# Rotated queries and keys of the second attention: transposed on TensorE, or in 32x32 blocks by VectorE with DMAs through device memory

## The chip, the cores and the metric

The kernel runs on one core of one Trainium2 chip. The metric is the device time of one execution, in microseconds (us). The kernel before takes 1788.93 us, the median of three runs (1788.12 to 1791.05).

## The reference

Two transformer blocks, one after the other, over 256 tokens of 2048 columns, all in float32. The change lies in the second block, where one wide product gives queries, keys and values of two attentions ("moba" and "dsa", eight heads of 128 each). Queries and keys are rotated before they are multiplied with each other:

```python
def _rope(x):                       # x: (1, T, heads, 128), T = 256
    half = dh // 2
    ang = arange(T)[:, None] * inv_freq[None, :]
    x1, x2 = x[..., :half], x[..., half:]
    return concatenate([x1 * cos(ang) - x2 * sin(ang), x2 * cos(ang) + x1 * sin(ang)], axis=-1)

proj = h @ w_in                     # 256 x 2048 times 2048 x 11344
ya = _moba_attention(_rope(qa), _rope(ka), va) @ w_moba_out
yb = _dsa_attention(_rope(qb), _rope(kb), vb, q_idx, k_idx, p_wi) @ w_dsa_out
y = (sigmoid(ga) * ya + sigmoid(gb) * yb) @ w_o
```

For each head the attention is softmax(q k^T / sqrt(128) + mask) v. TensorE sums over the partitions of both its operands, so q k^T needs queries and keys with the head's 128 features on the partitions. The projection leaves them with tokens on the partitions. Something has to transpose them, and that is what the change replaces.

## The kernel before

**Products.** Every product of activations with weights is made of three matmuls: each float32 operand is split into a high part, which the matmul takes as it is, and the rest, and high x high, high x low and low x high are summed (`three`, L1539 to L1542). The weights pass in *units* of 512 KB: two blocks of 128 rows by 512 columns. Eight units make a *turn*, in which one block of 512 output columns is made for both tiles of 128 tokens. The program has 76 turns, so 608 units, of 12 matmuls each. A turn's result lies in two PSUM banks, one for each token tile (`PAIR_A` or `PAIR_B`, in alternation).

**The path of a unit.** SyncE (SP) loads it into one of four slots of `raw` (L372), once VectorE is done with the unit four before it (semaphore `lo_ready`). ScalarE (ACT) writes the high part `w_hi` (L562), once TensorE (PE) is done with the unit four before it (`mm_done`). VectorE (DVE) subtracts and writes `w_lo` (L971). Then PE may start. In the programs of ACT and DVE the split of a unit stands three units ahead of PE's (`AHEAD = 3`): in the loop round s of a turn they split unit s + 3, and units 0 to 2 of the next turn are split in rounds 5 to 7.

**The groups.** The heads of both attentions go in four groups g = 0 to 3 of four heads. A group has three turns: queries (part 0, in `PAIR_B`), keys (part 1, `PAIR_A`), values (part 2, `PAIR_B`), that is turns 16 + 3g, 17 + 3g and 18 + 3g. At the end of parts 0 and 1, DVE rotates the result (`rope_chunk`, then `rope`): per token tile two products into `rope_a`, two into `rope_b`, two sums into `rot` (L1271, L1273, L1279). In the next turn, after PE's unit 3, PE turns the 2 x 4 blocks of 128 x 128 of `rot` into two banks (`turn_qk`, through `turn_rows`, L1586), and ACT copies them to `q2_t` or `k2_t` (`keep_qk`, L825). The attention of group g, `attn2(g, k)`, stands between the units 1 to 6 of the following turn, which is part 0 of group g + 1, or the first gate turn. Its first instruction on PE waits for `qk_ready`.

**What sets the order.** Everything is written out by hand: each engine has its own program, in the order in which the functions are called, and semaphores join them. DMAs are issued by SP (weights and all that concerns the kernel's own buffers) and GpSimd (POOL: `ada_raw`, the modulation weights, 512 KB each, which DVE adds up in L978). An engine's waits stand in its program, so all that is behind a wait waits too. That is so on SP as well: a DMA's wait is made before it is issued, and the loads behind it come later.

**The same way elsewhere.** In the feed-forward stage a 256 x 512 result goes this way already: DVE transposes it in 32x32 blocks (L1478), SP writes it to `f_home` in device memory (`write_f`, L436, a row of 4 KB per partition), and reads it back with the blocks in their places (`read_f`, L444, four DMAs of 128 KB in runs of 1 KB). The write is issued after the load of unit 1 of a turn and the read after that of unit 4.

## Time and profile before

| what | value |
| --- | --- |
| median of three runs | 1788.93 us |
| the profiled execution, its own time | 1789.1 us |
| its span in the trace | 1787.4 us |
| TensorE busy | 1772.0 us, 99% |
| VectorE busy | 1255.9 us, 70% |
| ScalarE busy | 898.2 us, 50% |
| GpSimd busy | 124.1 us, 7% |
| granted TensorE clock | 0.999 of full speed (2.4 GHz) |
| share of DMA engines busy in 40 slices | 0.5 to 0.9 |

The span is the time from the program's first instruction to its last. The median was 0.2 us under the profiled execution's time, so differences read from the trace can be set against either. The groups stand in the span from about 421 us (queries of group 0) to about 710 us; their last attention ends in the first gate turn, near 730 us.

### The profile page before, as it was taken

The page shows a single profiled execution, that of the slowest core. Times are in us where ns is not written, and L with a number is a line of the kernel's source. Part 1 is how long each engine was busy: PE and PEld are TensorE (multiplying, and loading weights), DVE is VectorE, ACT ScalarE, POOL GpSimd, SP SyncE. Part 2 cuts the span into 40 slices and gives each one's busy share as a digit, 9 for nine tenths or more (in the row PEclk, how much of TensorE's full clock was granted, in tenths as well). Part 3 has the DMA queues.
Part 4 walks back from the last instruction along what each step waited for, and adds up shares of the span by engine and source line. Part 5 has one row for each costly group of instructions (what it writes and reads, how often), then busy time and mean ns, then how long its engine had stood idle before and what let it go on. Part 6 is the DMA issues. An engine that isn't in the chain of part 4 may idle for free.

```text
span 1787.4 us, 25539 instructions
## 1 busy us (share of the span) xinstructions
PE 1772.0 (99%) x8266; PEld 1456.0 (81%) x8266; DVE 1255.9 (70%) x1685; ACT 898.2 (50%) x1273; POOL 124.1 (7%) x217
## 2 busy tenths in 40 slices
PE   9999999999999999999999999999999999999998
PEld 7777778887888888888888888888888888888886
DVE  5677779778877877777677868777775654545545
ACT  6766675545445454544444545444444444444443
POOL 1011101010000000210001101000000000000000
PEclk9999999999999999999999999999999999999999
DMA  9778778555667768698888966999998865555554
GB/s 354 250 260 282 237 279 314 205 186 172 212 216 243 245 212 293 208 319 284 283 282 289 308 224 211 333 307 319 315 294 241 237 220 191 195 192 193 193 191 139
DMA packets 192894, 443.78 MB, mean 248 GB/s; under 512 B 16849, under 2 KB 25537, under 8 KB 192449
## 3 DMA queue, kind: packets, MB, share of 16 engines
q1 hardware_dynamic: 164384, 339.08, 58.1%
q0 software_dynamic: 28304, 103.89, 17.8%
q8 instruction: 34, 0.56, 0.1%
q14 instruction: 28, 0.22, 0.0%
q10 hardware_dynamic: 144, 0.03, 0.0%
HBM read 432.46 MB, written 10.49 MB: 248 GB/s over the span
## 4 chain that ended last, share of the span: by engine, by line
PE 95%; DMA 2%; DVE 2%; ACT 1%; SPq 0%; issue 0%; DVEq 0%; ACTq 0%
PE bank L1540 30%; PE bank L1542 30%; PE bank L1541 30%; DMA raw<-in_w_in_a 2%; PE bank L1586 1%; PE bank L1710 1%; PE bank L1693 1%; DVE w_lo L971 0%; PE bank L1803 0%; PE bank L1685 0%; PE bank L1809 0%; PE bank L1682 0%; DVE x L998 0%; PE bank L1566 0%; ACT y L566 0%; PE bank L1815 0%
## 5 line engine op out<-in xcount | busy, mean ns | idle before, releaser
L971 DVE TENSOR_TENSOR w_lo<-raw,w_hi 128x1024 fp32r<-128x1024 f32 x605 | 728.9, 1210 | 415.4 <-ACT w_hi L562 413.6
L562 ACT ACTIVATE w_hi<-raw 128x1024 fp32r<-128x1024 f32 x605 | 633.4, 1050 | 709.0 <-PE bank L1542 653.3
L1540 PE MATMUL bank<-w_hi,h_hi 128*128 128x512 f32 x2272 | 895.8, 394 | 3.4 <-DVE w_lo L1081 1.8
L1542 PE MATMUL bank<-w_hi,h_lo 128*128 128x512 f32 x2272 | 885.3, 390 | 0.0
L1541 PE MATMUL bank<-w_lo,h_hi 128*128 128x512 f32 x2272 | 884.5, 389 | 0.0
L1540 PEld LDWEIGHTS bank<-w_hi,h_hi 128*128 128x128 f32 x2272 | 426.7, 188 | 95.5 <-issue 7.2
L1542 PEld LDWEIGHTS bank<-w_hi,h_lo 128*128 128x128 f32 x2272 | 426.5, 188 | 90.2
L1541 PEld LDWEIGHTS bank<-w_lo,h_hi 128*128 128x128 f32 x2272 | 427.0, 188 | 85.1
L978 DVE SCALAR_TENSOR_TENSOR acc_a<-ada_raw,cond,acc_a 128x1024 f32<-128x1024 f32 x112 | 143.3, 1279 | 12.1 <-DMA ada_raw<-in_w_ada 11.9
L487 POOL DMA_DIRECT2D ada_raw<-in_w_ada x160 | 84.7, 529 | 955.7 <-DVE acc_a L978 710.0
L978 DVE SCALAR_TENSOR_TENSOR acc_b<-ada_raw,cond,acc_b 128x1024 f32<-128x1024 f32 x48 | 64.3, 1340 | 1.3 <-DMA ada_raw<-in_w_ada 1.3
L1540 PE MATMUL bank<-w_hi,o_hi 128*128 128x512 f32 x128 | 49.8, 389 | 0.0
L1541 PE MATMUL bank<-w_lo,o_hi 128*128 128x512 f32 x128 | 49.8, 389 | 0.0
L1542 PE MATMUL bank<-w_hi,o_lo 128*128 128x512 f32 x128 | 49.8, 389 | 0.0
L1163 DVE CUSTOM_DVE_ANT_0 s<-bank,bias 128x128 f32<-128x128 f32 x64 | 20.2, 354 | 33.6 <-issue 21.1
L715 ACT ACTIVATE s<-s,neg_cur 128x128 f32<-128x128 f32 x32 | 12.8, 401 | 31.1 <-DVE neg_cur L1168 30.9
L1540 PEld LDWEIGHTS bank<-w_hi,o_hi 128*128 128x128 f32 x128 | 24.0, 188 | 5.0
L1541 PEld LDWEIGHTS bank<-w_lo,o_hi 128*128 128x128 f32 x128 | 24.0, 188 | 5.0
L1542 PEld LDWEIGHTS bank<-w_hi,o_lo 128*128 128x128 f32 x128 | 24.0, 188 | 5.0
L923 ACT ACTIVATE acc_b<-bank 128x512 f32<-128x512 f32 x32 | 19.2, 600 | 17.5 <-PE bank L1542 17.5
L1478 DVE STREAM_TRANSPOSE acc_b<-acc_b 128x512 f32<-128x512 f32 x32 | 22.8, 712 | 1.1
L487 POOL DMA_DIRECT2D ada_more<-in_w_ada x32 | 16.9, 528 | 84.4 <-DVE acc_a L978 44.4
(206 smaller groups left out, 938.1 us busy)
## 6 DMA issues: line engine op xcount, KB each, us to landing
raw<-in_w_ff SPq DMA_DIRECT2D x256, 512.0 KB, 4.5
raw<-in_w_in SPq DMA_DIRECT2D x176, 512.0 KB, 4.5
ada_raw<-in_w_ada POOLq DMA_DIRECT2D x160, 512.0 KB, 5.0
raw<-in_w_in_a SPq DMA_DIRECT2D x69, 512.0 KB, 5.3
ada_more<-in_w_ada POOLq DMA_DIRECT2D x32, 512.0 KB, 6.0
raw<-in_w_out_a SPq DMA_DIRECT2D x32, 512.0 KB, 5.6
raw<-in_w_o SPq DMA_DIRECT2D x32, 512.0 KB, 5.6
raw<-in_w_moba SPq DMA_DIRECT2D x16, 512.0 KB, 4.3
```

The lines of the kernel that those rows point to most:

```text
L487: pool.dma_start(two(ada_slot(slot), 1), w_ad[:, bass.ds(k, 1), col:col + D // 2])\
L562: act.activation(used(w_hi, turn, s), used(raw, turn, s), ACT.Copy).then_inc(hi_ready, 1)
L923: act.activation(f_tok[:, t, :], pair[p][t][:, :], ACT.Relu).then_inc(evicted[p][t], 1)
L971: dve.tensor_tensor(used(w_lo, turn, s), used(raw, turn, s), used(w_hi, turn, s).bitcast(F32), ALU.subtract).then_inc(lo_ready, 1)
L978: dve.scalar_tensor_tensor(part, ada_slot(slot), cond[:, bass.ds(k, 1)], part, ALU.mult, ALU.add)\
L1163: ins = dve.tensor_tensor_reduce(s1[:, j % 2, c0:c1], banks[SCORES + j % 2][:, c0:c1], bias1[:, j % 2, c0:c1], 1.0, LOWEST, ALU.add, ALU.m ...
L1478: dve.transpose(by_quadrant[:, t], f_tok[:, t, :]).then_inc(f_blocked, 1)
L1540: pe.matmul(out_ap, hi, rhs_hi, start=start, stop=False)
L1541: pe.matmul(out_ap, hi, rhs_lo, start=False, stop=False)
L1542: return pe.matmul(out_ap, lo, rhs_hi, start=False, stop=stop)
L1586: ins = pe.transpose(dst[:, b * P:(b + 1) * P], src[:, t, b * P:(b + 1) * P], ident)
L1693: pe.matmul(banks[OUTS][lane, at:at + SEQ], v1_cur[:, 0, :], p1_t[:, n, 0:SEQ], start=True, stop=False)
```

## The change

It takes out the 64 PE transposes (`turn_qk`) and the 16 ACT copies (`keep_qk`). In their place, for each n = 0 to 7 (n = 2g queries, n = 2g + 1 keys of group g):

- DVE, right behind the rotation, transposes the two token tiles of `rot` in 32x32 blocks into `rope_ab`. That is the buffer whose halves are now `rope_a` and `rope_b`, the rotation's own scratch. So the next rotation may begin only when the write of this one to device memory has landed (`rot_written`).
- SP writes `rope_ab` to `rot_home[n]`. Keys go in one DMA, with rows of 4 KB. Queries go in four DMAs of 32 partitions, in runs of 32 numbers, that is 128 bytes: 1024 runs each.
- SP reads it back into `q2_t` or `k2_t` in four DMAs of 32 partitions. For queries the runs are of 512 bytes, for keys of 1 KB.
- `k2_t` then holds the keys in another order, and PE reads them with strides, in runs of 32 numbers (`keys_of_head`). `q2_t` looks as before.

The places: queries are written behind the load of unit 2 of the values' turn and read behind that of unit 5. Keys are written behind the load of unit 1 of the turn after the values' turn and read behind unit 4. SP's loops over the groups are written out.

```diff
+ROT_WRITES = 16 * (QUADS + 1)
-                rope_a = sb("rope_a", [P, CH], on=a2)
-                rope_b = sb("rope_b", [P, CH], on=a2)
+                rope_ab = sb("rope_ab", [P, T * CH], on=a2)
+        rope_a, rope_b = rope_ab[:, 0:CH], rope_ab[:, CH:2 * CH]
+        rot_home = nc.dram_tensor("rot_home", (2 * HEADS_2 // 2, P, T * CH), F32, kind="Internal").ap()
...
+            def write_rot(n):
+                sp.wait_ge(rot_blocked, n * T + T)
+                if n % 2:
+                    sp.dma_start(rot_home[n], rope_ab[:, :]).then_inc(rot_written, 16)
+                else:
+                    homes = rot_home[n].rearrange("a b -> (a b)").rearrange("(q c i r) -> i c q r", c=QUAD, i=QUADS, r=QUAD)
+                    for i in range(QUADS):
+                        sp.dma_start(homes[i], rope_ab[i * QUAD:(i + 1) * QUAD, :].rearrange("c (q r) -> c q r", r=QUAD))                            .then_inc(rot_written, 16)
+            def read_rot(n):
+                if n < 2:
+                    sp.wait_ge(i_scores, IDX_HEADS)
+                else:
+                    sp.wait_ge(s2_ready, n // 2 * 4)
+                if n:
+                    sp.wait_ge(qk_loaded, n * 16 * QUADS)
+                sp.wait_ge(rot_written, n // 2 * ROT_WRITES + (ROT_WRITES if n % 2 else 16 * QUADS))
...
+                for j in range(QUADS):
+                    sp.dma_start(dst[j * QUAD:(j + 1) * QUAD], homes[j]).then_inc(qk_loaded, 16)
+            def load_with_rot(turn, col, n, at):
+                for s in range(UPT):
+                    load(turn, s, w_2[:, KG * s:KG * s + KG, col:col + CH])
+                    if s == at:
+                        write_rot(n)
+                    if s == at + 3:
+                        read_rot(n)
...
-            def keep_qk(n, dst):
-                for t in range(T):
-                    act.wait_ge(qk_turned, n * T + t + 1)
-                    act.activation(dst[:, :, t * P:t * P + P], two(banks[TURNED + t][:, :], 4), ACT.Copy)\
-                        .then_inc(qk_ready, 1)
...
             def rope_chunk(p, turn, use, n):
                 for t in range(T):
                     chunk_result(t, turn, turn)
                     rope(pair[p][t][:, :], rot[:, t, :], evicted[p][t], use, t, n, 4, DH_2 // 2, C_COS, C_SIN)
+                for t in range(T):
+                    dve.wait_ge(rot_ready, n * T + T)
+                    dve.transpose(rot_by_quadrant[:, t], rot[:, t, :]).then_inc(rot_blocked, 1)
...
-                    dve.wait_ge(qk_turned, g * 2 * T)
+                    dve.wait_ge(rot_written, g * ROT_WRITES)
                 rope_chunk(PAIR_B, g * 3 + TURN_GRP, g * 2 + 7, g * 2 + 3)
...
-                dve.wait_ge(qk_turned, g * 2 * T + T)
+                dve.wait_ge(rot_written, g * ROT_WRITES + 16 * QUADS)
                 rope_chunk(PAIR_A, g * 3 + TURN_GRP + 1, g + 9, g * 2 + 4)
...
-            def turn_qk(n):
-                for t in range(T):
-                    pe.wait_ge(rot_ready, (n + 3) * T + t + 1)
-                    turn_rows(rot, t, 4, banks[TURNED + t], qk_turned)
+            def keys_of_head(k):
+                flat = k2_t[:, :, :].rearrange("p b n -> p (b n)")
+                return flat.rearrange("p (i b t r) -> p b t i r", i=QUADS, b=CH // P, t=T)[:, k]
...
-                        pe.wait_ge(qk_ready, (g + 1) * 2 * T)
+                        pe.wait_ge(qk_loaded, (g + 1) * (2 * 16 * QUADS))
```

On SP, after the change, this stands in the turns 17 to 19 (the first row holds loads up to unit 2 of the values' turn 18). `raw` is a weight load, `rot_home` a write of the rotated block, `q2_t` and `k2_t` the reads; the semaphores that a row waits for are in brackets.

```order
121 L375 DMA raw<-in_w_in_2 128x2x512 [waits lo_ready] x20
122 L429 DMA rot_home<-rope_ab 32x32x32 [waits rot_blocked]
123 L429 DMA rot_home<-rope_ab 32x32x32 x3
124 L375 DMA raw<-in_w_in_2 128x2x512 [waits lo_ready] x3
125 L445 DMA q2_t<-rot_home 32x8x128 [waits rot_written,i_scores]
126 L445 DMA q2_t<-rot_home 32x8x128 x3
127 L375 DMA raw<-in_w_in_2 128x2x512 [waits lo_ready] x4
128 L425 DMA rot_home<-rope_ab 128x1024 [waits rot_blocked]
129 L375 DMA raw<-in_w_in_2 128x2x512 [waits lo_ready] x3
130 L445 DMA k2_t<-rot_home 32x4x256 [waits rot_written,qk_loaded,i_scores]
131 L445 DMA k2_t<-rot_home 32x4x256 x3
```

Before, SP had nothing but weight loads there. The 13 DMAs of a group now stand among them, in the same queue, and the loads behind rows 125 and 130 also wait for `rot_written`.

On DVE, the rotation of the queries in the loop over g = 1 to 3, before the change (`bank2` and `bank3` are `PAIR_B`, the two token tiles):

```order
567 L971 TENSOR_TENSOR w_lo<-raw,w_hi 128x1024 [waits hi_ready]
568 L976 REGISTER_ALU [waits ada_loaded1]
569 L978 SCALAR_TENSOR_TENSOR acc_a<-ada_raw,cond,acc_a 128x1024 [waits ada_done]
570 L1359 ISA
571 L1269 ISA [waits front_done,qk_turned]
572 L1271 TENSOR_TENSOR rope_a<-bank2,consts 128x4x64 [waits rot_ready]
...
582 L1279 TENSOR_TENSOR rot<-rope_a,rope_b 128x4x64 [waits evicted_b1]
583 L1279 TENSOR_TENSOR rot<-rope_a,rope_b 128x4x64
584 L970 REGISTER_ALU
585 L971 TENSOR_TENSOR w_lo<-raw,w_hi 128x1024 [waits hi_ready]
```

And the same place after the change:

```order
569 L1000 TENSOR_TENSOR w_lo<-raw,w_hi 128x1024 [waits hi_ready]
570 L1005 REGISTER_ALU [waits ada_loaded1]
571 L1007 SCALAR_TENSOR_TENSOR acc_a<-ada_raw,cond,acc_a 128x1024 [waits ada_done]
572 L1392 REGISTER_ALU
573 L1298 ISA [waits front_done,rot_written]
574 L1300 TENSOR_TENSOR rope_ab<-bank2,consts 128x4x64 [waits rot_ready]
...
585 L1308 TENSOR_TENSOR rot<-rope_ab 128x4x64
586 L1356 REGISTER_ALU
587 L1357 STREAM_TRANSPOSE rope_ab<-rot 128x4x4x32 [waits rot_ready] x2
588 L999 REGISTER_ALU
589 L1000 TENSOR_TENSOR w_lo<-raw,w_hi 128x1024 [waits hi_ready]
```

Two block transposes stand between the rotation and the split of the next turn's unit 3, and the wait ahead of the rotation is for a DMA's landing instead of for PE. The keys' rotation has moved in the same way.

## Rows read from the trace of the kernel before

**Rows 1.** The page: busy time of TensorE, and the chain by engine.

```profile
PE 1772.0 (99%) x8266; PEld 1456.0 (81%) x8266; DVE 1255.9 (70%) x1685; ACT 898.2 (50%) x1273; POOL 124.1 (7%) x217
...
PE 95%; DMA 2%; DVE 2%; ACT 1%; SPq 0%; issue 0%; DVEq 0%; ACTq 0%
```

**Rows 2.** Waits of TensorE, whole span: in total, times, longest (us).

```profile
PE bank L1540 <- DVE w_lo L1081: 1.8, 3, 0.8
```

**Rows 3.** Timeline of TensorE, values' turn of group 1: start, duration, instruction.

```profile
545.41 0.39 PE L1542 MATMUL bank<-w_hi,h_lo 128*128 128x512 f32 x1
...
548.13 0.39 PE L1542 MATMUL bank<-w_hi,h_lo 128*128 128x512 f32 x1
548.36 1.03 PE L1586 MATMUL bank<-consts,rot 128*128 128x128 f32 x8
...
551.29 0.39 PE L1540 MATMUL bank<-w_hi,h_hi 128*128 128x512 f32 x1
```

**Rows 4.** Timeline of VectorE, feed-forward: a block transpose and the instruction behind it.

```profile
1126.33 0.71 DVE L1478 STREAM_TRANSPOSE acc_b<-acc_b 128x512 f32<-128x512 f32 x1
1126.96 1.19 DVE L971 TENSOR_TENSOR w_lo<-raw,w_hi 128x1024 fp32r<-128x1024 f32 x1
```

**Rows 5.** Timeline of ScalarE: its copies wait for the end of TensorE's units.

```profile
449.20 1.06 ACT L562 ACTIVATE w_hi<-raw 128x1024 fp32r<-128x1024 f32 x1 [1.66 <-PE bank L1542]
...
472.04 1.06 ACT L562 ACTIVATE w_hi<-raw 128x1024 fp32r<-128x1024 f32 x1 [1.66 <-PE bank L1542]
...
523.18 1.06 ACT L562 ACTIVATE w_hi<-raw 128x1024 fp32r<-128x1024 f32 x1 [1.66 <-PE bank L1542]
...
545.84 1.06 ACT L562 ACTIVATE w_hi<-raw 128x1024 fp32r<-128x1024 f32 x1 [1.66 <-PE bank L1542]
```

**Rows 6.** Timeline of VectorE: first splits behind rotations, and the keys' rotation of group 1.

```profile
447.69 1.22 DVE L971 TENSOR_TENSOR w_lo<-raw,w_hi 128x1024 fp32r<-128x1024 f32 x1
...
520.44 2.35 DVE L971 TENSOR_TENSOR w_lo<-raw,w_hi 128x1024 fp32r<-128x1024 f32 x2
...
538.47 0.75 DVE L1271 TENSOR_TENSOR rope_a<-bank,consts 128x256 f32<-128x256 f32 x2
...
542.84 2.35 DVE L971 TENSOR_TENSOR w_lo<-raw,w_hi 128x1024 fp32r<-128x1024 f32 x2
```

**Rows 7.** Timeline of SP: loads of unit 2 (groups 0, 1), then 5 and 6.

```profile
455.10 0.37 SPq L372 DMA_DIRECT2D raw<-in_w_in  x1
...
526.43 0.37 SPq L372 DMA_DIRECT2D raw<-in_w_in  x1
...
534.89 0.37 SPq L372 DMA_DIRECT2D raw<-in_w_in  x1
...
537.51 0.37 SPq L372 DMA_DIRECT2D raw<-in_w_in  x1
```

**Rows 8.** Busy time from 521 to 526 us: PE, PEld, DVE, ACT, POOL, clock, DMA share, GB/s.

```profile
521.00:526.00 5.00, 5.00 (x25) 4.13 (x24) 5.00 (x5) 1.68 (x3) 0.53 (x1) 1.00 0.58 179
```

**Rows 9.** DMA from 370.8 to 371.8 us: one load of 80 KB in packets of 320 bytes.

```profile
q1 hardware_dynamic: 272, 0.08, 35.6%
```

**Rows 10.** DMA from 526 to 542 us (values' turn of group 1); q0 is POOL's.

```profile
q1 hardware_dynamic: 1722, 3.30, 58.6%
q0 software_dynamic: 509, 1.89, 36.4%
...
raw<-in_w_in SPq DMA_DIRECT2D x5, 512.0 KB, 5.5
```

**Rows 11.** DMA from 454 to 466 us (values' turn of group 0).

```profile
raw<-in_w_in SPq DMA_DIRECT2D x5, 512.0 KB, 4.2
```

**Rows 12.** DMA issues of the whole span: count, KB each, median us to landing.

```profile
f_home<-acc_b SPq DMA_DIRECT2D x16, 512.0 KB, 6.5
f_t<-f_home SPq DMA_DIRECT2D x64, 128.0 KB, 4.6
```

**Rows 13.** Line L1803: duration in ns, minimum, median, maximum.

```profile
L1803 PE MATMUL bank<-k_t,q_t x32: 379/380/382, 492.0 to 725.2; 128*128 128x256 f32 x32
```

More of the change, by code:

```diff
@@ L295, in two_block_kernel @@
         mask_ready = sem("mask_ready")
-        qk_turned = sem("qk_turned")
-        qk_ready = sem("qk_ready")
+        rot_blocked = sem("rot_blocked")
+        rot_written = sem("rot_written")
+        qk_loaded = sem("qk_loaded")
         mask_set = sem("mask_set")
@@ L418, in _ @@
                 load(TURN_KI, s, w_2[:, k:k + KG, col:col + cols])
-            for half in range(2):
-                with sp.Fori(0, 2) as b:
-                    for part in range(3):
-                        load_chunk((b + 2 * half) * 3 + TURN_GRP + part, w_2,
-                                   b * CH + (half * 3 + part) * W2)
-            load_chunk(TURN_GATE, w_2, COL_GA)
+            def write_rot(n):
[6 more added lines that the diff above has]
+                        sp.dma_start(homes[i], rope_ab[i * QUAD:(i + 1) * QUAD, :].rearrange("c (q r) -> c q r", r=QUAD))                            .then_inc(rot_written, 16)
@@ new lines, in read_rot @@
+            def read_rot(n):
[6 more added lines that the diff above has]
+                sp.wait_ge(rot_written, n // 2 * ROT_WRITES + (ROT_WRITES if n % 2 else 16 * QUADS))
+                if n % 2:
+                    dst = k2_t[:, :, :].rearrange("p b n -> p (b n)").rearrange("p (i n) -> p i n", i=QUADS)
+                    homes = rot_home[n].rearrange("(i f) (j n) -> j f i n", i=QUADS, j=QUADS)
+                else:
+                    dst = q2_t[:, :, :].rearrange("p b (t m) -> p (b t) m", t=T)
+                    homes = rot_home[n].rearrange("a b -> (a b)").rearrange("(j q c m) -> j c q m", j=QUADS, c=QUAD, m=P)
+                for j in range(QUADS):
+                    sp.dma_start(dst[j * QUAD:(j + 1) * QUAD], homes[j]).then_inc(qk_loaded, 16)
@@ new lines, in load_with_rot @@
+            def load_with_rot(turn, col, n, at):
[5 more added lines that the diff above has]
+                        read_rot(n)
+            for g in range(4):
+                for part in range(3):
+                    turn, col = g * 3 + TURN_GRP + part, g % 2 * CH + (g // 2 * 3 + part) * W2
+                    if part == 2:
+                        load_with_rot(turn, col, 2 * g, 2)
+                    elif part == 0 and g:
+                        load_with_rot(turn, col, 2 * g - 1, 1)
+                    else:
+                        load_chunk(turn, w_2, col)
@@ L425, in _ @@
+            load_with_rot(TURN_GATE, COL_GA, 7, 1)
             load_chunk(TURN_GATE + 1, w_2, COL_GB)
@@ L1320, in _ @@
             dve.wait_ge(w_idx_ready, T)
+            rot_by_quadrant = rope_ab[:, :].rearrange("p (j b t r) -> p t b j r", j=QUADS, b=CH // P, t=T)
             def rope_chunk(p, turn, use, n):
@@ L1801, in attn2 @@
                     bank = banks[SCORES + k % 2]
-                    pe.matmul(bank[:, 0:P], q2_t[:, k, 0:P], k2_t[:, k, 0:P], start=True, stop=True)
-                    pe.matmul(bank[:, P:MASK_W], q2_t[:, k, P:SEQ], k2_t[:, k, :], start=True, stop=True)\
-                        .then_inc(s2_ready, 1)
+                    key = keys_of_head(k)
+                    pe.matmul(bank[:, 0:P], q2_t[:, k, 0:P], key[:, 0], start=True, stop=True)
+                    pe.matmul(bank[:, P:MASK_W], q2_t[:, k, P:SEQ], key, start=True, stop=True).then_inc(s2_ready, 1)
                 if k >= 2:
```

9 lines of the change are left out of this document (removed).

## The prediction

> **What bounds the kernel now.** I read the page first. TensorE is busy for 99% of the span and is 95% of the chain that ended last [rows 1]. Its list of waits is nearly empty: the longest entry for VectorE's weight splits is 1.8 us in all [rows 2]. So a microsecond taken from TensorE's program counts in full, and so does one in which TensorE waits for something new. The change does both kinds of thing: it takes instructions from TensorE, and it puts work and a wait into VectorE's program, ahead of splits that TensorE needs. So the rest of my reading is of spare time: by how much is each split early, and how long does a DMA take there.
>
> **What goes.** In the timeline of TensorE a unit's 12 matmuls take 545.41 to 548.13, so 0.227 us each. From the matmul at 548.13 to the one at 551.29, ten matmuls later, 2.27 us would be due. It takes 3.16 us, since eight transposes stand between [rows 3]. They cost 0.89 us, and `turn_qk` runs 8 times: 7.1 us. ScalarE also loses its 16 copies. That is worth nothing, since its weight copies wait for TensorE for 1.66 us each [rows 5].
>
> **What VectorE gets.** A block transpose of 128 x 512 starts 0.63 us before the instruction behind it [rows 4]. Two of them, and about 0.1 us (an estimate) until the rotation's last result is written, cost 1.4 us per rotation, 8 times. Are they hidden? ScalarE's copy for unit u + 3 starts as TensorE ends unit u - 1, so its start is also TensorE's start of unit u. For the queries of group 1 the first split behind the rotation (unit 3) ends at 520.44 + 1.22 = 521.66 [rows 6], and TensorE takes that unit at 523.18 [rows 5]: 1.5 us to spare, 1.4 needed. For the keys it ends at 544.06 and is needed at 545.84: 1.8 to spare. So groups 1 to 3 hide the transposes, and nothing more than 0.1 and 0.4 us is left. In group 0, whose DVE also does the selection of the index scores, the split ends at 448.91 and is needed at 449.20: 0.3 us to spare, so the queries' transposes there cost 1.1 us.
>
> **The new wait.** The rotation of the keys writes its scratch into `rope_ab`, which still holds the queries' block, and so waits until the four DMAs of 128-byte runs have landed. Behind it on VectorE are the two rotations and the split of unit 3, for which TensorE waits. When is the write issued, and by when must it land?
>
> Group 1 stands for 1 to 3. The load of unit 2 is issued at 526.43 [rows 7]. VectorE's splits release it, and VectorE is busy without a gap ahead of it (5.00 of 5 us) [rows 8], so the transposes push it 1.4 us back, to 527.8. The write follows 0.4 us later, at 528.2. The keys' rotation started at 538.47, and from there to the end of the first split are 5.6 us [rows 6]. With 1.4 us for the transposes the rotation must start 7.0 us before 545.84 - 0.9 (TensorE is sooner by one set of transposes) = 544.9, so at 537.9. The write has 9.7 us.
>
> How long does it take? A load issued here lands after 5.5 us, and the DMA engines are full: SP's queue has 58.6% and POOL's 36.4% of them [rows 10]. The load of unit 2 stands ahead of the write in the same queue, so the write begins to move in earnest about 5.1 us after its issue. It has 4096 packets of 128 bytes, 256 for each of 16 engines. No row shows such packets. The nearest are 256 packets of 320 bytes (with 16 of semaphores): they kept 16 engines busy for 35.6% of 1 us, 21 ns each [rows 9]. By count of packets the write then takes 256 x 21 ns = 5.4 us. By bytes it would take 2.3 us (0.08 MB in 0.356 us of full share). I take the count. Beside it POOL's queue gets its turn: 5.8 us for 3.6 loads [rows 10] is 1.6 us for each, and 1.3 of them fall in: 2.1 us. Sum: 5.1 + 5.4 + 2.1 = 12.6 us. The write of `f_home`, with the same bytes in 128 packets, gives the same by another way: 6.5 us [rows 12], less its own 1.5 (3.30 MB take 58.6% of 16 us), plus 7.5, is 12.5. So VectorE starts 2.9 us late, and TensorE waits for that long, three times: 8.7 us.
>
> In group 0 the load of unit 2 is issued at 455.10 [rows 7], 1.4 later after the change, and the write at 456.9. Loads land in 4.2 us there and POOL is quiet [rows 11]: 3.8 + 5.4 = 9.2, so it lands at 466.1. The split is needed at 472.04 [rows 5] - 0.9 + 1.1 = 472.2, so the rotation must start at 465.2. That costs 0.9 us.
>
> **What is behind the write on SP.** The weight loads of units 3 to 5 queue behind its packets, and SP itself waits before the read, from about 535 on, when the load of unit 5 has gone (534.89) [rows 7], until the write has landed at 540.8. The load of unit 6, which was issued at 537.51 [rows 7], then comes about 5 us late with the four reads ahead of it. ScalarE took that unit at 545.84 [rows 5], which is 2.8 us after it landed (5.5 us after its issue), and TensorE three units later, some 6 us after VectorE's split of it, so there are about 9 us. The keys' write is like the one of `f_home`, 6.5 us, and is issued three loads (8 us) ahead of its read; the reads land in 4.6 us each [rows 12], some 7 us after the first is issued. TensorE needs them before unit 2 of that turn. A load comes 16.5 us before TensorE takes its unit (537.51 for unit 6 [rows 7], which TensorE reaches three units of 2.72 us after 545.84 [rows 5]), so the attention is 11 us behind the load of unit 4. I cost them at nothing. If that cover were gone, TensorE would wait at the first head's scores.
>
> **Strided keys.** The 256-column matmul of scores takes 0.38 us, 32 times [rows 13]. Nothing in the trace shows a moving operand in runs of 32 numbers. From below it costs nothing. From above, if each such row of 128 bytes made it twice as long, the 32 would cost 12 us. I take nothing, since the number of columns is the same.
>
> **The sum.** -7.1 (TensorE's transposes) + 1.1 (transposes in group 0) + 0.9 + 8.7 (the wait) = +3.6 us. On the profiled execution's 1789.1 us this is 1792.7; the median is 0.2 lower, so 1792.5.
>
> **Where the page and the row differ.** The row gives 21 ns for a packet of 320 bytes read from device memory [rows 9]; it says nothing of writes. The Trainium skill, "DMA: Bandwidth & Descriptors", section Specifications, says that below 512 bytes a transfer does not run at line rate, since the engine reads, modifies and writes. By this rule the write would be dearer than my count, and that is the second rival below. Another section of it (Bandwidth, Measured) has about 10.5 ns as the least time of a packet; by that figure the write would be an estimated 2.7 us, and the sum would be that of the first rival.
>
> **Rival 1: the write lands in time.** If packets cost by their bytes, 2.3 us + 1.6 for one load of POOL + 5.1 = 9.0 us, under the 9.7 that are free. Group 0 has 6.1 against 8.3. Then only 1.1 us of the gain is lost: -6.0, so 1783. For it: the engines moved 320-byte packets at 230 GB/s of full share. Against it: the 1722 packets of SP's queue, nearly all of 2 KB, kept the engines busy for 87 ns each (58.6% of 16 us times 16) [rows 10]. At that pace 320 bytes would take 14 ns and not 21, so the packet itself costs something.
>
> **Rival 2: short writes are slow.** The place is the same wait. Twice the row's 21 ns, a read and a write for each packet, would be 42 ns [rows 9]. At 30 ns the write moves for 7.7 + 2.5 us and lands after 15.3: 5.6 us late, three times, and group 0 loses 3.2 + 1.1: -7.1 + 21.1 = +14, so 1803. At 42 ns it lands after 19.1 us: 28.2 + 6.3 + 1.1 - 7.1 = +28.5, so 1817. It decides from about 24 ns on. Middle: 1808. Then loads queued behind the write would be late as well, at about the same point, so the two do not add up.
>
> **Rival 3: another place.** The keys' reads land after the first head's scores, or strided keys are slow. With 2 us each, four times, it is 8 more: 1798 or above. Against it: the margin of 4 us above.
>
> **Chances.** A run tells a difference of about 0.2%, 3.6 us, from none. My forecast (packets of 17 to 24 ns, 1788 to 1797, middle 1792.5): 0.40. Rival 1 (1782 to 1787): 0.31. Rival 2 (1800 to 1818): 0.24. Rival 3: 0.05. Faster than 1785.3 is most of rival 1 (0.31 with the edge of mine). Within 0.2% lie a small part of rival 1 and half of mine: 0.25. Slower: 0.44. Range, with 2 in 10 left out, most of it above: 1782 to 1813.
>
> **What would show it.** TensorE's busy transposes of `rot` fall from 64 to none in this stretch. The landing of the `rot_home` writes of queries: about 12.6 us by my count, 9 by rival 1, over 15 by rival 2. TensorE's wait for `w_lo` behind the keys' rotation, in each group at unit 3 of the values' turn: 2.9 us, none, or over 5. VectorE waits ahead of the keys' rotation for the DMA of `rot_home`. SP waits for it ahead of the reads. The prediction is wrong if TensorE shows no wait there, if it waits at unit 3 for loads (`w_hi` released by a DMA), or if waits of TensorE turn up in the attention.

## The result, and the profile after

| | before | after |
| --- | --- | --- |
| median | 1789.39 us (7 runs, 1788.12 to 1791.05) | 1801.53 us (7 runs, 1794.13 to 1807.76) |
| profiled execution, span | 1787.4 us | 1799.8 us |
| TensorE idle, 430 to 745 us | 0.0 us | 14.1 us |
| granted clock at half speed there | none | twice 3.4 us |

The change makes the kernel slower: the ratio is 1.0065, with an interval of 1.0052 to 1.0079, that is +11.6 us (9.3 to 14.1). The time lies in the predicted range and on the predicted side; the predicted 1792.5 was 9 us too low. The executions of the changed kernel also differ more, by 13.6 us where those of the kernel before differ by 2.9. The two fastest (1794.13 and 1795.20) had a mean granted clock of 0.999, the slowest 0.996. The trace below is of one execution, of 1801.65 us.

The page, with the lines that answer to [rows 1]. TensorE's busy time is only 0.5 us smaller, though 64 transposes are gone; 6.8 us at half clock give back about half of what they took. DMAs, VectorE and SP have taken 10 points of the chain from TensorE.

```profile
PE 1771.5 (98%) x8202; PEld 1452.4 (81%) x8202; DVE 1265.7 (70%) x1701; ACT 889.6 (49%) x1257; POOL 124.1 (7%) x217
...
PE 84%; DMA 6%; DVE 6%; SPq 2%; ACT 1%; issue 1%; DVEq 0%; ACTq 0%
```

TensorE's waits between 430 and 745 us, where the kernel before has none: us in all, times, longest.

```profile
PE bank L1573 <- DVE w_lo L1000: 7.6, 4, 2.8
PE bank L1573 <- ACT v L881: 4.9, 2, 2.9
PE bank L1835 <- DMA k_t<-rot_home: 1.5, 2, 0.9
```

That is three kinds. The first holds the two that I had priced: 1.17 us behind the block transposes of group 0, and three stalls at unit 3 of the values' turn. The timeline of VectorE in group 1, with the start, duration, instruction and in brackets the idle time before it and its releaser, shows the wait for the queries' write, as foreseen; it answers to [rows 6].

```profile
539.94 0.76 DVE L1300 TENSOR_TENSOR rope_ab<-bank,consts 128x256 f32<-128x256 f32 x2 [2.12 <-DMA rot_home<-rope_ab]
...
544.44 1.30 DVE L1357 STREAM_TRANSPOSE rope_ab<-rot 128x512 f32<-128x512 f32 x2
545.66 2.31 DVE L1000 TENSOR_TENSOR w_lo<-raw,w_hi 128x1024 fp32r<-128x1024 f32 x2
```

The second kind I had not foreseen. The first unit of the turn behind the values' turn needs the banks that ScalarE copies the values from (L881). TensorE's and ScalarE's timelines there:

```profile
563.75 0.79 PE L1573 MATMUL bank<-w_hi,h_hi 128*128 128x512 f32 x1 [2.95 <-ACT v L881]
564.34 0.63 PE L1574 MATMUL bank<-w_lo,h_hi 128*128 128x512 f32 x1
...
567.47 0.40 PE L1573 MATMUL bank<-w_hi,h_hi 128*128 128x512 f32 x1
```

```profile
558.38 1.06 ACT L600 ACTIVATE w_hi<-raw 128x1024 fp32r<-128x1024 f32 x1 [4.43 <-DMA raw<-in_w_in]
562.16 1.06 ACT L600 ACTIVATE w_hi<-raw 128x1024 fp32r<-128x1024 f32 x1 [2.72 <-DMA raw<-in_w_in]
563.12 1.06 ACT L881 ACTIVATE v<-bank 128x512 f32<-128x512 f32 x2
```

ScalarE copies the values behind its split of unit 2 of the next turn, and that split waited for its weights. In the kernel before, the same split runs at 557.61 with its load long there, and waits for TensorE instead:

```profile
557.61 1.06 ACT L562 ACTIVATE w_hi<-raw 128x1024 fp32r<-128x1024 f32 x1 [1.66 <-PE bank L1542]
558.97 0.60 ACT L852 ACTIVATE v<-bank 128x512 f32<-128x512 f32 x1 [0.30 <-PE bank L1542]
```

After the stall the matmuls start 0.43 us apart, not 0.23: the clock is at its level of 1.2 GHz. In the columns of [rows 8], for the stretches from 563 and 642 us:

```profile
563.00:570.00 7.00, 6.25 (x21) 5.03 (x22) 5.14 (x5) 4.58 (x6) 0.56 (x2) 0.76 1.06 308
642.00:650.00 8.00, 8.00 (x29) 6.51 (x30) 4.58 (x5) 3.81 (x4) 1.05 (x2) 0.79 1.04 338
```

A mean of 0.76 over 7 us costs 1.7 us, 0.79 over 8 us the same. So: 14.1 us of stalls, 3.4 us of half clock, less 7.7 us of transposes (first experiment), make +9.8 of the 12.4 us between the spans. By an estimate, 1.3 us more lie at the edges of the eight stalls: a matmul here lasts 0.39 us and the next one starts 0.23 us after it, and ahead of a stall the 0.16 us between the two are not shared. The last 1.3 us I did not place.

Why is the weight load late? ScalarE's waits in the same stretch, before and then after. These rows show best what has changed:

```profile
ACT w_hi L562 <- PE bank L1542: 98.9, 63, 1.7
...
ACT w_hi L562 <- DMA raw<-in_w_in: 6.3, 3, 2.4
```

```profile
ACT w_hi L600 <- DMA raw<-in_w_in: 95.2, 45, 5.9
ACT w_hi L600 <- PE bank L1575: 33.2, 22, 1.8
```

Before, ScalarE waited for weights 3 times in 315 us. After, 45 times: the weights often arrive just as they are needed, or later. The landing times from 545 to 562 us, before and after, in the columns of [rows 10]:

```profile
raw<-in_w_in SPq DMA_DIRECT2D x7, 512.0 KB, 4.9
ada_raw<-in_w_ada POOLq DMA_DIRECT2D x4, 512.0 KB, 4.9
```

```profile
raw<-in_w_in SPq DMA_DIRECT2D x6, 512.0 KB, 8.4
ada_raw<-in_w_ada POOLq DMA_DIRECT2D x3, 512.0 KB, 7.8
rot_home<-rope_ab SPq DMA_DIRECT2D x1, 512.0 KB, 9.4
k_t<-rot_home SPq DMA_DIRECT2D x4, 128.0 KB, 5.0
```

The six weight loads of the last view by themselves:

```profile
DMA to landing us min/median/max: 4.7/8.4/12.4
```

Landing time is not all of it. The load of unit 2 behind the values' turn, for which ScalarE waits at 562.16, lands at 562.05; in the kernel before it landed at 554.33. Of these 7.7 us, 4.3 are its longer way (9.8 us, not 5.5). The other 3.4 stand ahead of its issue (552.23, not 548.82), for which SP waits until VectorE has done the split that frees the slot. VectorE's splits run late here: behind the rotation by the transposes and the scratch wait (545.66, not 542.84), and further on by waits for loads.

And the engines' share and rate, 22 us each, two stretches before and then the same after:

```profile
530.00:552.00 22.00, 22.00 (x103) 18.31 (x102) 18.41 (x24) 8.98 (x10) 2.11 (x4) 1.00 0.84 287
552.00:574.00 22.00, 22.00 (x104) 18.42 (x103) 14.23 (x29) 12.05 (x19) 1.58 (x3) 1.00 0.84 264
```

```profile
530.00:552.00 22.00, 20.25 (x89) 16.44 (x88) 17.32 (x24) 6.81 (x8) 1.59 (x4) 1.00 1.07 304
552.00:574.00 22.00, 19.05 (x78) 15.37 (x77) 13.29 (x18) 9.44 (x14) 2.11 (x4) 0.92 0.99 329
```

The DMA engines went from 0.84 of their time to all of it.

### The profile page after: what moved, and what is told of

It reads as the page before. It is cut to its first block, busy times and chain, and to the rows that moved or that the text cites. A ratio compares the mean times of both kernels' runs of the same rounds, so it can differ in the third digit from the quotient of the medians.

```text
span 1799.8 us, 25163 instructions
## 1 busy us (share of the span) xinstructions
PE 1771.5 (98%) x8202; PEld 1452.4 (81%) x8202; DVE 1265.7 (70%) x1701; ACT 889.6 (49%) x1257; POOL 124.1 (7%) x217
## 4 chain that ended last, share of the span: by engine, by line
PE 84%; DMA 6%; DVE 6%; SPq 2%; ACT 1%; issue 1%; DVEq 0%; ACTq 0%
PE bank L1573 26%; PE bank L1575 26%; PE bank L1574 26%; DVE w_lo L1000 2%; DMA raw<-in_w_in 2%; DMA raw<-in_w_in_a 2%; DMA rot_home<-rope_ab 1%; SPq L429 1%; DMA k_t<-rot_home 1%; PE bank L1743 1%; PE bank L1619 1%; DVE rope_ab L1300 1%; DVE rope_ab L1302 1%; PE bank L1726 1%; ACT w_hi L600 1%
## 5 line engine op out<-in xcount | busy, mean ns | idle before, releaser
L1573 PEld LDWEIGHTS bank<-w_hi,h_hi 128*128 128x128 f32 x2272 | 427.9, 188 | 109.6 <-DVE w_lo L1000 12.6
L753 ACT ACTIVATE s<-s,neg_cur 128x128 f32<-128x128 f32 x32 | 12.8, 401 | 31.1 <-DVE neg_cur L1197 30.9
L1376 DVE CUSTOM_DVE_ANT_0 s<-bank,mask_cur 128x128 f32<-128x128 f32 (+1 forms) x32 | 10.2, 356 | 19.4 <-PE bank L1836 19.4
```

What stands on the lines that cost most here:

```text
L1573: pe.matmul(out_ap, hi, rhs_hi, start=start, stop=False)
```

## The experiments

The first four kernels were made to part theories of what the DMAs cost: VectorE's wait for the shared scratch (A), the short runs, which hold SP (B), and the extra traffic itself, which makes weight loads land late (C). After e5 and e6 theory D was added, that several costs are covered alone and only together are not. The twelve kernels in one table. "Traced" is the time of the profiled execution, from which the columns behind it are taken; all in us but "late". "Idle" is TensorE's idle time from 430 to 745 us, "weights" ScalarE's wait for `raw` there, "late" how many of the about 100 weight loads there landed more than 8 us after their issue, "half" the time at 1.2 GHz there.

| kernel | median | ratio to before | traced | idle | weights | late | half |
| --- | --- | --- | --- | --- | --- | --- | --- |
| before | 1789 | | 1789.1 | 0.0 | 6.3 | 1 | 0 |
| after | 1801.53 | 1.0052 to 1.0079 | 1801.65 | 14.1 | 95.2 | 18 | 6.8 |
| e1 no transposes at all | 1781.72 | 0.9941 to 0.9974 | 1784.27 | 0.3 | 18.4 | 3 | 0 |
| e2 after, long runs | 1799.52 | 1.0045 to 1.0079 | 1799.36 | 10.5 | 84.3 | 30 | 6.8 |
| e3 after, own buffers | 1801.45 | 1.0055 to 1.0088 | 1802.18 | 13.3 | 76.6 | 16 | 13.7 |
| e4 keys only | 1796.22 | 1.0019 to 1.0044 | 1798.58 | 8.6 | 32.6 | 17 | 3.4 |
| e5 before + transfers | 1789.76 | 0.9996 to 1.0014 | 1791.88 | 1.4 | 43.5 | 9 | 0 |
| e6 after, thin modulation | 1784.63 | 0.9968 to 0.9987 | 1785.55 | 2.4 | 63.1 | 3 | 0 |
| e7 keys only, later | 1791.70 | 1.0009 to 1.0029 | 1793.84 | 4.7 | 27.9 | 16 | 3.4 |
| e8 after, all eased | 1800.48 | 1.0048 to 1.0076 | 1801.69 | 13.0 | 77.3 | 25 | 6.8 |
| e9 before + block transposes | 1791.31 | 1.0004 to 1.0022 | 1792.37 | 1.2 | 23.9 | 0 | 0 |
| e10 before + both | 1793.76 | 1.0018 to 1.0039 | 1796.83 | 3.2 | 56.3 | 10 | 3.4 |
| e11 after, early copy | 1806.26 | 1.0087 to 1.0117 | 1801.64 | 13.4 | 80.0 | 16 | 10.2 |
| e12 keys only, early copy | 1797.30 | 1.0034 to 1.0061 | 1797.93 | 8.9 | 23.7 | 17 | 6.8 |

The runs of before that stand beside them have medians of 1789.38 (e1 to e4), 1788.69 (e5 to e8) and 1788.89 (e9 to e12). The traced execution can be far from the median: e10's is the slowest of eight and e4's the slowest of six, e11's the fastest of four.

**e1: what the transposes are worth.** The kernel before without `turn_qk`, `keep_qk` and the waits for them.

```diff
-                    if s == 3:
-                        pe.wait_ge(o2_kept, g * 4 + 1)
-                        turn_qk(g * 2)
...
-                    if s == 4:
-                        keep_qk(g * 2, q2_t)
```

> The kernel before, with turn_qk and keep_qk left out: nothing fills q2_t and k2_t, so the attention works on what the index scores left there. It gives the worth of TensorE's 64 transposes alone. By the count from the timeline (0.89 us each of 8 times) 1789.4 - 7.1 = 1782.3 us. If the transposes lay partly in time that TensorE would have waited anyway, the gain is smaller, 3 to 5 us; if the copies of ScalarE slowed TensorE too, it is larger, 8 to 9.

Measured 7.7 us less than before (4.7 to 10.6). The term of 7.1 stands. TensorE is sooner by this much, and so wants its weights sooner: ScalarE's wait for them grows from 6.3 to 18.4 us, with a single stall of 0.3 us.

**e2: long runs.** Queries are written like keys, in rows of 4 KB, and read like them, so their order is not the one that the attention needs.

```diff
-                    for i in range(QUADS):
-                        sp.dma_start(homes[i], rope_ab[i * QUAD:(i + 1) * QUAD, :].rearrange("c (q r) -> c q r", r=QUAD))
...
+                sp.dma_start(rot_home[n], rope_ab[:, :]).then_inc(rot_written, 16)
```

> The changed kernel, but the queries are written as the keys are, in one DMA with rows of 4 KB, and read back in runs of 1 KB (their order in q2_t is then another one). The bytes are the same, the 4096 short packets of a write are gone. Theory A (the keys' rotation waits for the queries' write) and theory B (SP is held while it issues the short-run DMAs, and the weight loads and the keys' write behind them come late) both expect that the cost goes: the write lands in some 6.5 us, under the 9.7 that are free; TensorE's waits in the groups fall from 14 us to about 1.1 (group 0) and the time is 1783 to 1785. Theory C (it is the 8 MB of extra traffic, whatever its packets) expects over 1790, with loads late in the values' turns.

The stalls at unit 3 shrink from 6.45 us to 1.17 (0.42, 0.26 and 0.49), but the time falls by 2 us only, which is inside the interval. The stalls behind the values stay (4.9 us, now 4.6) and those for the keys' read have grown from 1.5 us:

```profile
PE bank L1564 <- ACT v L872: 4.6, 2, 3.7
PE bank L1826 <- DMA k_t<-rot_home: 3.5, 2, 2.1
PE bank L1564 <- DVE w_lo L991: 2.3, 4, 1.2
```

So the short runs do make the wait that I predicted, and taking it away gives nearly nothing back.

**e3: no shared scratch.** The rotation's scratch and the keys' block get buffers of their own, so VectorE never waits within a group for the queries' write. To make room, the load of `post_gain` goes behind the groups; e5, e8 and e10 have this too.

```diff
+        own_ab = (post_gain[:, 0:CH], post_gain[:, CH:2 * CH])
+        key_ab = post_gain[:, 2 * CH:4 * CH]
...
-                dve.wait_ge(rot_written, g * ROT_WRITES + 16 * QUADS)
```

> The changed kernel, but the rotation's scratch and the keys' transposed block have places of their own (in post_gain, whose own contents are loaded after the groups instead of before), so nothing on VectorE waits for the queries' write; SP's part is the same. Theory A alone: all of the cost hangs on that wait, so the time falls to 1783 to 1786. Theory A and B together: the waits at unit 3 of the values' turns (6.5 us) go, and those at the unit 2 of the next turn (4.9 us), at the first scores (1.6 us) and the half clock behind them (up to 3.4 us) stay, so 1793 to 1796.

No change: 1801.45, which neither expectation had. TensorE still stalls at unit 3 of the values' turn in groups 2 and 3, for 1.83 and 1.50 us (1.89 and 2.81 in the changed kernel), with no scratch to wait for: ahead of the rotation of group 2 VectorE waits 2.01 us for a high part, whose load is late. The largest stall is now 5.35 us at the first scores of the last group.

**e4: keys alone.** Queries stay with TensorE, so there are no short runs and half the traffic.

```diff
-                    if part == 2:
-                        load_with_rot(turn, col, 2 * g, 2)
-                    elif part == 0 and g:
-                        load_with_rot(turn, col, 2 * g - 1, 1)
+                    if part == 0 and g:
+                        load_with_rot(turn, col, g - 1, 1)
```

> Half of the change: the keys go by 32x32 blocks and DMAs (rows of 4 KB, runs of 1 KB), the queries stay with TensorE and ScalarE as before. No short runs, no wait of a rotation for a write. Theories A and B: gain of half the transposes, 3.6 us, and nothing lost, since the keys' block transposes have 1.8 us to spare: 1785.5 to 1786.5. Theory C: the traffic of the keys alone costs something, 1788 or more. If the strided keys were slow on TensorE it would show here too, in L1835 and L1836's durations; they are the same in the changed kernel's trace, so nothing is expected.

Still slower than before by 5.5 us (3.4 to 7.9), with the stalls of the second kind in full:

```profile
PE bank L1570 <- ACT v L878: 6.6, 2, 3.4
PE bank L1837 <- issue: 1.5, 1, 1.5
PE bank L1837 <- DMA k_t<-rot_home: 0.6, 1, 0.6
```

Neither A nor B is in this kernel at that place. From 545 to 562 us its weight loads land after 9.6 us. That is what theory C says.

**e5: the traffic alone.** The kernel before, with the same eight writes and reads at the same places of SP's queue, from a constant and into a buffer unused at that time. The writes wait for no engine.

```diff
+                        if part == 2 and s == 2:
+                            traffic(2 * g)
+                        if part == 2 and s == 5:
+                            query_read(2 * g)
+                        if part == 0 and g and s == 1:
+                            key_write(2 * g - 1)
+                        if part == 0 and g and s == 4:
+                            key_read(2 * g - 1)
```

> The kernel before, with TensorE's transposes kept, to which SyncE's queue adds the same eight writes (four of them in 128 B runs) and eight reads, at the same places between the weight loads, but from a constant and into a buffer that nothing uses: no engine waits for them. It tells the transfers' own cost from the cost of the waits that hang on them. If what costs is the transfers in the queue ahead of the weight loads (theory C), the last two loads behind each write land 4 to 5 us later, TensorE stalls 2 to 3 us at the first units of the turns after the values' and its clock halves there, and the time is 1794 to 1798. If what costs is the waits of VectorE and TensorE for the transfers (the theory of the prediction), nothing is seen and the time is 1788 to 1791.

Theory C in this plain form fails: +0.9 us, not told from nothing. The landings are late all the same, 7.1 us for the weights against 4.9, and ScalarE waits for them 43.5 us against 6.3:

```profile
ACT w_hi L603 <- PE bank L1583: 64.4, 44, 1.7
ACT w_hi L603 <- DMA raw<-in_w_in: 43.5, 22, 5.1
```

But TensorE waits only 1.4 us. The transfers alone eat a reserve and hardly any time.

**e6: more bandwidth.** The changed kernel, in which the 32 modulation loads of GpSimd inside the groups bring 256 of 1024 columns, so that part of the modulation is computed from stale weights.

```diff
-                load_tiles(g * 8 + 64, GT1, g * 4)
+                for n in range(8):
+                    load_half(g * 8 + 64, n, g * 4 + n // 2)
```

> The changed kernel with GpSimd's modulation loads inside the groups cut to 256 of their 1024 columns: the modulation is computed from partly stale weights, all instructions and waits stay. It takes about 8 MB off the DMA engines in the groups. If the engines' bandwidth in the burst behind each rotation is what makes the weight loads late (theory C), the loads (22, 2) and (22, 4) land within 7 us of their issue, the stalls at the first units after the values' turn (2.95 and 1.96 us) and both stretches of half clock go, those at the values' fourth unit shrink, and the time is 1786 to 1791. If it is SyncE's program, held while it issues the runs of 128 B, or the order of the work on ScalarE, the stalls stay and the time is 1798 to 1802.

16.9 us fewer than after, and below the kernel before. (The bytes taken off are 32 x 0.39 = 12.6 MB; the expectation had that too low.) SP's queue, the short runs, the shared scratch and ScalarE's order are all as in the changed kernel. What is left of TensorE's waits:

```profile
PE bank L1579 <- DVE w_lo L1006: 1.9, 2, 1.2
PE bank L1841 <- DMA k_t<-rot_home: 0.3, 1, 0.3
```

Only 3 loads are late, not 18, and VectorE's wait for the queries' write has shrunk from 6.2 us to 0.6. So crowded DMA engines are a necessary part of the loss. Which of the late transfers costs most, this kernel does not part. No run thins the loads of the kernel before; but that has no idle time in the groups that thinner loads could give back, so I put the 16.9 us down to the change.

**e7 and e8: later.** In e7, e4's keys are written behind the load of unit 2 and read behind unit 5, and the attention stands one unit later. In e8 the whole change is eased in this way, with own buffers, and the queries' four writes each behind a load of its own, from unit 7 of the keys' turn on.

```diff
-                    if s == at:
+                    if s == 2:
                         write_rot(n)
-                    if s == at + 3:
+                    if s == 5:
                         read_rot(n)
...
-                    if 1 <= s <= 6:
-                        attn2(g, s - 1)
+                    if 2 <= s <= 7:
+                        attn2(g, s - 2)
```

> As the kernel in which TensorE keeps the queries' transposes and the keys alone go over device memory (1796.2 us), but the keys' write is issued behind the third weight load of the values' turn's successor instead of the second, its read behind the sixth, and the attention's units stand one unit later. If the keys' write costs because it stands in the queue ahead of the load on which ScalarE waits before it copies the values (theory C, in the form of order), that load is no longer behind it: the stalls of 3.15 and 3.42 us go and the time is 1785 to 1789. If the bytes cost wherever they are, the stalls move to a later unit and the time is 1793 to 1797.

> The whole change with every suspected wait eased at once: rotation scratch and keys' block in buffers of their own, the queries' four writes issued one behind each of four successive weight loads, the keys' write and read one load later, the attention one unit later. If order and bursts are the cause, the time is 1782 to 1789, since 7.6 us of transposes are off TensorE. If the bytes cost wherever they are, it is 1793 to 1800.

e7 is 3.4 us slower than its runs of before where e4 is 5.5 slower than its own (the medians are 4.5 us apart, and the two intervals overlap). It falls between the two expectations: the stalls behind the values are gone and 3.8 us at scores have come. e8 gains nothing on e3. So where only the keys travel, order may be a small part of the loss; with all the traffic, easing places does not help.

**e9 and e10: the parts in the kernel before.** e9 adds VectorE's block transposes alone. e10 adds them and the transfers, each write issued once the blocks stand ready.

```diff
+                for t in range(T):
+                    dve.wait_ge(rot_ready, n * T + T)
+                    dve.transpose(rot_by_quadrant[:, t], rot[:, t, :]).then_inc(rot_blocked, 1)
```

> The kernel before, with TensorE's transposes kept and no transfer added, in which VectorE transposes each rotated half in 32x32 blocks into the rotation's scratch as in the change; nothing reads the blocks. It delays VectorE's next split, and so the slots and the loads, by 2.2 us after each rotation. By theory D (VectorE's 2.2 us and the added transfers are each covered alone, and only together make the loads late) TensorE waits no more than the 1.2 us of the first queries' rotation and the time is 1788 to 1791. If VectorE's delay alone is the cause, the stalls at the first units after the values' turn are seen here too, and the time is 1793 to 1798.

> The kernel before, with TensorE's transposes kept, plus both: VectorE's block transposes, and the eight writes and eight reads, each write issued once the blocks stand ready, from a constant, so that VectorE never waits for a write and TensorE never for a read. Theory D: loads land late, TensorE stalls 4 to 9 us in the groups, its clock halves at least once, and the time is 1794 to 1800. If the waits for the transfers themselves make the loss (VectorE's for the queries' write, TensorE's for the keys' read), none of it is here and the time is 1788 to 1791.

e9 costs 2.3 us (0.7 to 3.9), with one stall of 1.2 us, in group 0. e10 costs 5.0 (3.2 to 7.0), with 1793.76 just under what theory D expected, with the first stall of the second kind and one stretch at half clock:

```profile
PE bank L1588 <- ACT v L896: 1.8, 1, 1.8
PE bank L1588 <- DVE w_lo L1015: 1.4, 2, 1.2
```

The parts alone make 0.9 + 2.3 = 3.2, against 5.0 together, and these intervals do not tell the two apart: that the parts cost more together than alone is not shown by e10. What is told apart is the next step: e10 less TensorE's transposes should be 1793.8 - 7.7 = 1786, and the whole change is 1801.5. The stall and the half clock above are those of the slowest of e10's eight executions.

**e11 and e12: ScalarE's order.** The values are copied one split sooner, in the changed kernel and in e4's.

```diff
-                for s in range(UPT):
+                for s in range(UPT - 1):
                     split(g * 3 + TURN_GRP + 2, s + AHEAD)
                 for t in range(T):
                     chunk_result(t, g * 3 + TURN_GRP + 2, g * 3 + TURN_GRP + 2)
                     act.activation(v2[:, t, :], pair[PAIR_B][t][:, :], ACT.Copy).then_inc(evicted[PAIR_B][t], 1)
+                split(g * 3 + TURN_GRP + 2, UPT - 1 + AHEAD)
```

> The changed kernel, in which ScalarE copies the values ahead of its split of the third unit of the turn that follows, not behind it: one split moves past two copies. If TensorE's stalls of 2.95 and 1.96 us at the first unit of that turn come from that split's wait for its late load, they go, and both stretches of half clock with them (1.7 us each): 1801.5 - 4.9 - 3.4 = 1793, between 1792 and 1796. If the late loads themselves are what TensorE ends up waiting for, the stalls move to the third or fifth unit of that turn or to the first scores and the time is 1798 to 1802.

> The kernel in which the keys alone go over device memory (1796.2 us, stalls of 3.15 and 3.42 us behind the values), with the same earlier copy of the values. If the copy's place is the cause, 6.6 us of stalls and one stretch of half clock (1.7 us) go: 1787 to 1789, which is 1 us under the kernel before. If the late loads are the cause wherever the copy stands, it is 1793 to 1797.

Both fail as cures. The stalls behind the values go, and come back at the first scores, which wait for the keys' read:

```profile
PE bank L1574 <- DVE w_lo L1001: 7.3, 4, 2.8
PE bank L1836 <- DMA k_t<-rot_home: 5.6, 3, 4.5
```

```profile
PE bank L1838 <- DMA k_t<-rot_home: 7.4, 2, 4.7
PE bank L1850 <- DVE s L1364: 1.0, 1, 1.0
PE bank L1838 <- issue: 0.4, 1, 0.4
```

e11 is even slower than after and above both its expectations; its trace, of an execution of 1801.64 us, does not hold what the other three (1806.14 to 1806.94) have more. e12 is not told from e4. The place of ScalarE's copy decides where TensorE stalls, not whether. No version of the change that computes the whole result beat the kernel before.

## Why the prediction was right in its sign and short by 9 us

**The sign was in part luck.** With the measured sizes of the four terms that were in the sum, it is -7.7 + 1.2 + 6.5 = 0.0 us: the forecast would have been no change. That the kernel is slower comes from what stood in it at nothing. The prediction also named signs by which it would be wrong, and one of them is there: waits of TensorE turn up in the attention (1.5 us).

**TensorE's transposes, -7.1.** Right: -7.7 in e1.

**Block transposes in group 0, +1.1.** Right: 1.17 us in the timeline, and again in e9 to e11. The transposes' own row has 0.69 us for one (0.71 in [rows 4]):

```profile
L1357 DVE STREAM_TRANSPOSE rope_ab<-rot x16: 668/690/712, 447.4 to 703.5; 128x512 f32<-128x512 f32 x16
```

**VectorE's wait for the queries' write, 0.9 + 8.7.** The wait and its place were right: the write lands 11.7, 11.9 and 12.8 us after its first issue in groups 1 to 3 (12.6 forecast), and TensorE stalls at unit 3 of the values' turn for 1.75, 1.89 and 2.81 us (2.9 forecast). In group 0 it lands after 8.3 us (9.2 forecast) and there is no stall. In all 6.45 us and not 9.6; and e2 and e3, which take the wait away, gain no time. That the landing time agrees is luck, since its parts were other ones. The sum had all four writes start at once. In the trace the fourth is issued 5.6 to 8.1 us after the first (5.7 in group 1) and lands 4.7 to 6.2 us after that. And a packet of 128 bytes took not 21 ns. From 459 to 463 us there is little else on SP's queue:

```profile
DMA packets 3786, 0.70 MB, mean 175 GB/s; under 512 B 3669, under 2 KB 3669, under 8 KB 3786
...
q1 hardware_dynamic: 3786, 0.70, 88.5%
```

88.5% of 16 engines in 4 us are 56.6 us for 3786 packets. With 87 ns for each of the 117 long ones, 12.7 ns are left for a short one. Rival 2, which needs 24 ns or more, is out by this number. Rival 1's price (2.3 us for 256 packets, 9 ns each) was nearer, yet the write came late: its issue was drawn out, and it shared full engines, with a share of 1.09 from 530 to 534 us. How much each of the two adds, no run parts.

```profile
530.00:534.00 4.00, 4.00 (x19) 3.31 (x18) 3.19 (x3) 1.16 (x2) 0.53 (x2) 1.00 1.09 323
```

The Trainium skill, "DMA: Bandwidth & Descriptors", section Specifications, says that a transfer under 512 bytes does not run at line rate, since the engine reads, modifies and writes. The trace agrees in that such packets are slow: 128 bytes in 12.7 ns are 10 GB/s for each engine, under half of the 24 GB/s of a 2 KB packet (87 ns). At the pace of the long packets 128 bytes would take 5.4 ns, and they took 2.3 times that. Whether a second pass or a fixed price for each packet makes this, no run tells; the doubling of 21 ns in rival 2 was wrong.

**"I cost them at nothing": the step that failed.** This was said of the keys' write, all the reads and the loads behind them on SP. SP's own hold-up was longer than thought: SP waits 9.9 us for the writes, and is kept up to 4.4 us in issuing one of 1024 runs. e5 has the same places in SP's queue and costs 0.9 us, so by itself this hold-up was covered. The late loads were not, once the rest came to it. I had checked each against the landing time of the kernel before, 5.5 us, in which the new traffic is not contained. With it the loads of units 2 and 4 behind the values' turn land 9.8 and 12.4 us after their issue (5.5 and 4.5 before) and are issued 3.4 and 1.1 us later, the cover is gone, and TensorE pays 4.9 us at the values' copies, 1.5 us at the first scores and 3.4 us at half clock. My rival 3 has about the right time, and its mechanism, late reads at the first scores, is the smallest of these.

The Trainium skill has the rule that bears on it: "DMA: Bandwidth & Descriptors", section "Issuing engines are not separate DMA queues", says that queues of different issuers share the same engines. e6 agrees: with GpSimd's loads made thinner, 3 of SP's loads landed after more than 8 us and not 18.

**The sum itself.** Its form was wrong too. I added stalls, each against its own cover, and the covers look like one reserve: how early the weights are. This is argued and not shown by a run of its own. ScalarE's wait for weights is one sign of how much of it is spent. Beyond the 6.3 us of before, the faster TensorE spends 12.1 (e1), the block transposes 17.6 (e9) and the transfers 37.2 (e5). Together that makes 73, and e3, which has all three and no scratch wait, shows 76.6. Alone they cause 0.3, 1.2 and 1.4 us of idle time, together 13.3. That would be why removing one wait (e2, e3, e11) gave nothing, and giving bandwidth back (e6) nearly all.

The total of ScalarE's waits is no measure across all kernels, though. e6 has 63.1 us of them and 2.4 us of idle time, e5 43.5 and 1.4, but e4 has 32.6 and 8.6, and e12 23.7 and 8.9. The count of loads that take over 8 us parts the kernels better: with 10 or fewer TensorE is idle for 3.2 us at most, with 16 or more for 4.7 us at least. An estimate says why that length matters. There are four slots, so a unit's load waits for the split of the unit four before it, and TensorE takes four units in 4 x 2.72 = 10.9 us. ScalarE's and VectorE's splits take 1.06 and 1.2 of these; so when loads that follow each other take longer than some 8.6 us, the stream falls behind TensorE.

**Strided keys, 0.** Right. The 256-column matmul of scores takes what it took in [rows 13]:

```profile
L1836 PE MATMUL bank<-k_t,q_t x32: 379/381/383, 491.9 to 737.6; 128*128 128x256 f32 x32
```

**Open.** e10 and e3 differ in two things, TensorE's and ScalarE's transposing work and the waits of TensorE for the reads; no run parts them. Some 1.3 us between the spans are not placed. Theory D rests on e3 against e5, e9 and e10, which differ in more than one thing, and on the estimate above; no chain of runs adds one cost at a time up to the changed kernel.

## What to carry to other kernels

Work that goes from a busy compute engine to DMAs is paid for in landing time of every transfer beside it; price it at the landing times with the new traffic in it, in the stretch where the engines are fullest, not at those of the profile before. Do not check each new cost against the whole margin of one stream of loads: costs that were covered alone (0.3, 1.2 and 1.4 us of idle time) were not covered together (13.3). Count the loads that take nearly as long as their slots are free (here 1, then 18 over 8 us), not only the median. When a stall that is removed comes back elsewhere, stop moving instructions and take load off what they all wait for.

## What the runs showed of the hardware

- SyncE is held while it issues DMAs of many short runs one behind another: four of 1024 runs of 128 bytes take 7.04 us of its program here, and one up to 4.4 us. The first of the four takes 0.47 us in three groups of four, as one with rows of 4 KB does. In e8, with a weight load ahead of each, none of the sixteen takes over 0.81 us. In e6, with the engines less crowded, one still takes up to 4.6 us.

```profile
528.08 7.04 SPq L429 DMA_DIRECT2D rot_home<-rope_ab x4
```

```profile
L430 SPq DMA_DIRECT2D rot_home<-rope_ab x16: 467/494/812, 449.6 to 678.3; - x16
```

- Of the clock: stalls of 1.96 and 2.95 us (after), 1.8 us (e10) and 3.67 us (e2) were followed by 3.4 us at 1.2 GHz, those of 4.47 (e11), 4.67 (e12), 5.15 (e8) and 5.35 us (e3) by 6.8 us, and stalls of 1.89 and 2.81 (after, groups 2 and 3) and 3.42 us (e4) by none. So in these runs a stall of 4.47 us or more cost 3.4 us more than itself, and one of 1.8 to 3.7 us cost 1.7 more or nothing.
- Short writes of 128 bytes and loads beside them move 175 GB/s with the engines 0.88 busy (from 459 us); with rows of 4 KB in their place (e2) it is 386 GB/s at 0.99.
